# One VectorE operation in place of two ScalarE operations for each expert row of tokens 256 to 511

## The chip, the core and the metric

The kernel runs on one core of a Trainium2 chip. The metric is the time of one execution on the device in microseconds (us); lower is better. The engines are named as in the profile: PE is TensorE (PEld its weight loads), DVE is VectorE, ACT is ScalarE, POOL is GpSimd, SP is SyncE, which issues most of the weight transfers.

## What is computed

Two transformer blocks over 512 tokens of width 1024, in fp32. The first ends in a layer that looks up experts: each token chooses 128 of 16,384 experts (8 heads times 16), and takes from each one a row of `expert_u` and one of `expert_v`. The second block is a differential attention, an MLP, a latent attention (MLA), an MLP and a norm. The change lies in the expert layer:

```
ue = jnp.take(expert_u, expert, axis=0)
ve = jnp.take(expert_v, expert, axis=0)
h = jax.nn.gelu(jnp.einsum('thkd,td->thk', ue, xc).astype(F32), approximate=False)
return jnp.einsum('thk,thkd->td', (gate * h).astype(xc.dtype), ve)
```

`gate` is the softmax over the chosen experts' scores. For every token and expert one needs a dot product of 1024, a gelu, a product with the gate, and a row of 1024 added to the token's sum with that weight.

## The kernel before, in words

**Rows.** The expert layer is cut into 512 "rows". Row n gathers 128 experts at once, one for each of the 128 SBUF partitions: a 1 MB tile, 1024 numbers of u and 1024 of v in each partition. For rows 0 to 255 a row is one expert slot of 128 tokens. For rows 256 to 511 ("stacked") a row holds four expert slots of each of 32 tokens. A row goes through five steps, each on its own engine:

1. POOL issues the gather (`pool_rows`, L1754), once the buffer is free, which it is when PE has used the row seven before (row n-7) in it.
2. DVE makes the dot products (`dve_dot`, L1892), with a wait for the gather and for the dot of row n-1. One instruction gives 128 dot products, as a column of the tile `dots`.
3. ACT applies gelu (L1847), multiplies by the gate (L1849, "the weight"), and writes a diagonal matrix of the weights (L1856 for stacked rows: 128 x 32, four 32 x 32 diagonals one above the other; L1859 with 128 x 128 for the others). Each has a wait for the one before it. All three stand in `act_weight`.
4. PE multiplies the diagonal with the row's v part (`pe_rows`; L1778 for stacked rows, four matmuls of 128 x 32 by 128 x 256, which the trace shows as eight records). This adds the weighted v rows to the sums in PSUM. It is called acc(n) here, and the instruction of step 2 dot(n).
5. After 128 rows the sums are moved out and joined to the residual.

**What runs beside the rows.** Rows 0 to 255 run beside the choice of experts. Rows 256 to 511 run beside the whole second block for tokens 0 to 255 ("half 0"), which is the stage of the change. The second half of the tokens follows with no rows beside it. Each engine's program is written by generators: `beside(stage, rows, rate)` takes a piece of the second block's code, then as many steps of the row generator as are due (1.1 for each unit of weight), then the next piece. The same cut is made on every engine, so that each engine's stream is a fixed interleaving of row steps and pieces, and every engine works through its own in order. A place between two pieces at which row steps stand is called a gap here; a gap has one step, sometimes two, in the MLP one or none beside the half-weight pieces and now and then three.

**The row steps.** In step s DVE does dot(s+1), ACT does the three operations of row s+1, and PE does acc(s-1) for the stacked rows (`late`, with LAG = 1). So PE's part of a row stands two steps behind DVE's and ACT's part. Where the engines keep level, that is the slack that a row has between its diagonal and its use.

**The weights of the second block.** Matmuls of the second block run on weights that are split into two parts. SP loads 512 KB to a `raws` buffer, ACT writes the high part (`act_hi`, L297, 128 x 1024, to `whs` or `whw`), POOL subtracts it from the weight to get the low part (`pool_lo`, L303, to `wls` or `wlw`). POOL's stream has the low parts and the gathers in one fixed order, so that a gather waits behind the low parts that stand ahead of it, and these wait for ACT's high parts. PE's matmuls of the second block are at L1998 (projections), L2557 and L2576 (the two halves of the MLP), L2239 and others.

**The attentions.** In `attention` each of 16 blocks of queries goes round the engines: PE makes the scores, DVE the maximum (L2482, for MLA L2939), ACT the exponential (L2391, for MLA L2827), DVE the softmax's division (L2496, for MLA L2948), PE turns the block and multiplies with v, ACT and DVE put the result away. Between gelu and exponential ACT loads another table (ACT_TABLE_LOAD).

Two more DVE lines are spoken of: L2048 writes a diagonal (128 x 128, from `ident` in SBUF to SBUF, by TENSOR_SCALAR), and L2484 scales a single column.

## Time and profile before

| | |
|---|---|
| Time, median of 3 runs | 3049.65 us (3047.44 to 3058.9) |
| Time of the profiled execution | 3047.7 us, its span 3045.9 us |
| Busy over the span | PE 85%, PEld 64%, POOL 54%, DVE 58%, ACT 46% |
| Granted clock of PE over the span | 0.927 |
| HBM traffic | 787.84 MB read, 261 GB/s over the span |
| Stage of rows 0 to 255 | about 610 to 1283 us of the span |
| Stage of the change, rows 256 to 511 beside half 0 | 1283 to 2310 us |
| Half 1 alone | 2310 us to the end |

The span is the time from the profile's first instruction to its last; the 1.8 us between it and the execution's time lie around it. Busy shares are means over stages with different limits, so that the stage of the change has to be read by itself. The "chain of waits" is the profile's way back from the last instruction: at each step to what released it, or to the instruction ahead of it on its engine. In this profile it reaches back to 1557 us and no further.

### The profile page before, as it was taken

Reading aid. Unit: us, or ns where it says so; the run is one execution under the profiler, and the core shown is the slowest. Engines: PE = TensorE matmul, PEld = TensorE weight load, DVE = VectorE, ACT = ScalarE, POOL = GpSimd, SP = SyncE. Lnnn points to the kernel's source line nnn. Section 1 sums busy time; section 2 is a strip of 40 time slices with the busy share of each in tenths; the row PEclk is TensorE's granted clock in tenths of the full one; section 3 lists DMA queues with packets and bytes.
Section 4 is the critical chain, followed back from the end, with each engine's and each line's share of the span. In section 5 each row is a group of like instructions: output and inputs, shape, how many; then the busy total and the mean of one; then the engine's idle time right before and its main releaser. Section 6 shows DMA issues by size and latency. Waiting matters only on the chain. (4 is left out here: it accounts for less than half of the span.)

```text
span 3045.9 us, 49365 instructions
## 1 busy us (share of the span) xinstructions
PE 2585.2 (85%) x18974; PEld 1960.1 (64%) x18974; DVE 1763.8 (58%) x3863; ACT 1388.3 (46%) x3129; POOL 1648.2 (54%) x973
## 2 busy tenths in 40 slices
PE   6997977987877777687698997679997999999998
PEld 3865965743333232265477776458776979989998
DVE  5686433767777776765654457565446463256323
ACT  2231222243344343456865456765554454444543
POOL 3822113834444443466287776358883618852785
PEclk8988978999999999888799998889997999999999
DMA  7210013289999999779789997989995415542453
GB/s 293 101 59 26 4 57 152 93 331 421 421 421 421 421 421 415 316 300 401 284 325 401 377 389 296 376 314 393 402 409 218 152 34 175 187 134 74 157 186 115
DMA packets 140538, 797.61 MB, mean 262 GB/s; under 512 B 15504, under 2 KB 18704, under 8 KB 67600
## 3 DMA queue, kind: packets, MB, share of 16 engines
q0 software_dynamic: 73728, 536.90, 43.4%
q1 hardware_dynamic: 65856, 253.09, 23.3%
q10 hardware_dynamic: 720, 4.46, 0.3%
q8 instruction: 151, 2.47, 0.3%
q14 instruction: 83, 0.68, 0.1%
HBM read 787.84 MB, written 6.55 MB: 261 GB/s over the span
## 5 line engine op out<-in xcount | busy, mean ns | idle before, releaser
L303 POOL TENSOR_TENSOR wls<-raws,whs 128x1024 fp32r<-128x1024 f32 (+1 forms) x256 | 612.0, 2400 | 370.3 <-ACT whs L297 368.3
L1998 PE MATMUL ps<-ts,whs 128*128 128x256 f32 x1424 | 292.2, 306 | 27.5 <-DVE ts L2093 19.6
L1754 POOL DMA_INDIRECT raw<-in_peer_uv,un x205 | 209.3, 1021 | 191.7 <-PE ps L1778 87.6
L297 ACT CAST whs<-raws 128x1024 fp32r<-128x1024 f32 (+1 forms) x256 | 263.9, 1036 | 96.8 <-PE ps L2576 35.2
L303 POOL TENSOR_TENSOR wlw<-raws,whw 128x1024 fp32r<-128x1024 f32 x112 | 267.8, 2404 | 70.4 <-ACT whw L297 69.7
L1847 ACT ACTIVATE un<-un 128x1 f32<-128x1 f32 x384 | 77.6, 202 | 445.6 <-DVE scratch L1892 432.0
L1998 PEld LDWEIGHTS ps<-ts,whs 128*128 128x128 f32 x1424 | 239.6, 205 | 56.1 <-issue 26.8
L1892 DVE SCALAR_TENSOR_TENSOR scratch<-raw,ps 128x1024 f32<-128x1024 f32 x149 | 181.4, 1217 | 133.4 <-DMA raw<-in_peer_uv,un 120.2
L2576 PE MATMUL ps<-ts,whs 128*128 128x256 f32 x1216 | 228.7, 289 | 0.2 <-DVE ts L2629 0.2
L1998 PE MATMUL ps<-ts,wls 128*128 128x256 f32 x712 | 209.8, 295 | 0.0
L303 POOL TENSOR_TENSOR wl<-raw,wh 128x2048 fp32r<-128x2048 f32 x23 | 107.1, 4660 | 186.0 <-ACT wh L297 186.0
L2576 PEld LDWEIGHTS ps<-ts,whs 128*128 128x128 f32 x1216 | 190.6, 193 | 19.8 <-issue 16.8
L2557 PE MATMUL ps<-ts,whs 128*128 128x256 f32 x1088 | 202.3, 287 | 0.0
L2557 PE MATMUL ps<-ts,whw 128*128 128x256 f32 x960 | 182.6, 291 | 9.5 <-DVE ts L2093 9.5
L2658 DVE TENSOR_TENSOR kept<-kept,ps 128x256 f32<-128x256 f32 x256 | 103.8, 418 | 129.4 <-PE ps L2576 129.3
L2557 PEld LDWEIGHTS ps<-ts,whs 128*128 128x128 f32 x1088 | 170.3, 193 | 12.8 <-issue 11.9
L2576 PE MATMUL ps<-ts,wls 128*128 128x256 f32 x608 | 172.8, 284 | 0.0
L2557 PEld LDWEIGHTS ps<-ts,whw 128*128 128x128 f32 x960 | 152.5, 195 | 22.2 <-DVE ts L2093 10.7
L1892 DVE SCALAR_TENSOR_TENSOR scratch<-raw,scratch 128x1024 f32<-128x1024 f32 x108 | 135.6, 1260 | 50.4 <-DMA raw<-in_peer_uv,un 26.1
L1754 POOL DMA_INDIRECT un<-in_peer_uv,un x104 | 105.2, 1011 | 108.7 <-PE ps L1782 51.6
L333 PE MATMUL ps<-uh,wh 128*128 128x512 f32 x368 | 149.3, 406 | 15.3 <-DVE ul L1281 5.3
L2622 DVE SCALAR_TENSOR_TENSOR ps<-ps,rs 128x256 f32<-128x256 f32 x128 | 55.2, 431 | 179.2 <-PE ps L2557 178.9
(443 smaller groups left out, 6883.2 us busy)
## 6 DMA issues: line engine op xcount, KB each, us to landing
raws<-in_w_up SPq DMA_DIRECT2D x128, 512.0 KB, 4.2
raws<-in_w_down SPq DMA_DIRECT2D x128, 512.0 KB, 4.7
scratch<-in_ada_w SPq DMA_DIRECT2D x17, 1024.0 KB, 13.2
raws<-in_w_qk SPq DMA_DIRECT2D x32, 512.0 KB, 8.5
raw<-in_w_in SPq DMA_DIRECT2D x11, 1024.0 KB, 5.3
raw<-in_peer_w_q SPq DMA_DIRECT2D x8, 1024.0 KB, 8.0
raws<-in_w_v SPq DMA_DIRECT2D x16, 512.0 KB, 5.7
raws<-in_w_o_a SPq DMA_DIRECT2D x16, 512.0 KB, 4.0
```

The costliest lines, as they stand in the source:

```text
L297: e.copy(self.wh[h][:, 0:width], self.raw[slot][:, 0:width]).then_inc(*self.tick("hi", key))
L303: e.tensor_tensor(self.wl[h][:, 0:width], self.raw[slot][:, 0:width], self.wh[h][:, 0:width].bitcast(F32), ALU.subtract).then_inc(*self.ti ...
L333: ins = e.matmul(self.ps[:, b, :], l, r, start=k == 0 and i == 0, stop=k == nk - 1 and i == 2)
L1754: e.indirect_dma_start(self.rows[r], None, self.d["peer_uv"], index).then_inc(*self.tick(f"row{r}", n, 16))
L1847: e.activation(gelus[:, c], dots[:, c], ACT.Gelu, bias=0.0, scale=1.0).then_inc(*self.tick(S))
L1892: e.scalar_tensor_tensor(out=self.junk[0 if n < 128 else n % 2 if n < 256 else 1], in0=self.rows[r][:, 0:1024], scalar=1.0, in1=xn, op0=AL ...
L1998: ins = e.matmul(o[:, 0:256], l, r, start=k == 0 and i == 0, stop=k == nk - 1 and i == 2)
L2557: ins = e.matmul(o[:, 0:256], l, r, start=k == 0 and n == 0, stop=k == 7 and n == 2)
L2576: ins = e.matmul(o[:, 0:256], l, r, start=t == 0 and n == 0, stop=t == 3 and n == 2)
L2622: e.scalar_tensor_tensor(out=x, in0=x, scalar=0.0, in1=H.rs, op0=ALU.max, op1=ALU.mult).then_inc(*self.tick(S, ("ready", g, t)))
L2658: e.tensor_tensor(x, x, self.bh((P_, "v", g, j)), ALU.add).then_inc(*self.tick(S, ("x", g, j)))
```

## The change

For stacked rows ACT now does the gelu alone. A new function, `dve_diagonal`, lets DVE write the diagonals with one `tensor_scalar`: the stack of unit diagonals (`each32`) times the gelu's column times the gate's column. It is called in DVE's row step n, behind dot(n+1), and waits for the gelu of row n and for acc(n-4), whose diagonal lay in the same buffer. PE's acc(n) now waits for DVE's diagonal instead of ACT's. Rows 0 to 255 are as before.

```
--- before.py
+++ after.py
@@ -1770,7 +1770,7 @@
                 b = 4 if tt == 0 else 6
                 if k == 0 and tt >= 2:
                     e.wait_ge(*self.at(A_, ("sums", tt - 1)))
-                e.wait_ge(*self.at(A_, ("diag", n)))
+                e.wait_ge(*self.at(D_ if self.stacked(n) else A_, ("diag", n)))
                 if self.stacked(n):
                     g = k // 32
                     for c in range(4):
@@ -1844,6 +1844,9 @@
         S, c, k = "peer_act", slice(n % 128, n % 128 + 1), n % 128
         dots, gelus, weight = self.dots[n >= 128], self.gelus[n >= 128], self.weight[n >= 128]
         e.wait_ge(*self.at("peer_dve", ("dot", n)))
+        if self.stacked(n):
+            e.activation(gelus[:, c], dots[:, c], ACT.Gelu, bias=0.0, scale=1.0).then_inc(*self.tick(S, ("gelu", n)))
+            return
         e.activation(gelus[:, c], dots[:, c], ACT.Gelu, bias=0.0, scale=1.0).then_inc(*self.tick(S))
         e.wait_ge(*self.last(S))
         e.activation(weight[:, c], gelus[:, c], ACT.Identity, bias=0.0,
@@ -1851,13 +1854,8 @@
         if n >= 4:
             e.wait_ge(*self.at("peer_pe", ("acc", n - 4)))
         e.wait_ge(*self.at(S, ("weight", n)))
-        diag = self.diag[n >= 128][n % 4]
-        if self.stacked(n):
-            e.activation(diag[:, 0:32], self.each32, ACT.Identity, bias=0.0,
-                         scale=weight[:, c]).then_inc(*self.tick(S, ("diag", n)))
-        else:
-            e.activation(diag, self.C("ident"), ACT.Identity, bias=0.0,
-                         scale=weight[:, c]).then_inc(*self.tick(S, ("diag", n)))
+        e.activation(self.diag[n >= 128][n % 4], self.C("ident"), ACT.Identity, bias=0.0,
+                     scale=weight[:, c]).then_inc(*self.tick(S, ("diag", n)))
 
     def act_join(self, e, tt):
         b = 4 if tt == 0 else 6
@@ -1871,10 +1869,20 @@
         for n in range(-1, 512 + LAG):
             if n + 1 < 512:
                 self.dve_dot(e, n + 1)
+            if 0 <= n < 512 and self.stacked(n):
+                self.dve_diagonal(e, n)
             if n in (130, 386 + LAG):
                 for j in range(8):
                     self.dve_join(e, n // 128 - 1, j)
             yield
+
+    def dve_diagonal(self, e, n):
+
+        k = n % 128
+        e.wait_ge(*self.at("peer_act", ("gelu", n)))
+        e.wait_ge(*self.at("peer_pe", ("acc", n - 4)))
+        e.tensor_scalar(self.diag[1][n % 4][:, 0:32], self.each32, self.gelus[1][:, k:k + 1], self.gate[n // 128][:, k:k + 1],
+                        ALU.mult, ALU.mult).then_inc(*self.tick("peer_dve", ("diag", n)))
 
     def dve_dot(self, e, n):
         S, r = "peer_dve", self.row_of(n)
```

The lines behind the change move by up to 8: DVE's dot is L1900 in the changed kernel, the gelu of stacked rows L1848, the new operation L1884, MLA's lines 2939, 2941, 2946, 2948 and 2954 are L2947, L2949, L2954, L2956 and L2962.

ACT's stream in the first MLP, before (`un` holds dots, gelus, weights, gates and diagonals of these rows; `kept` the unit diagonals; `whs` and `whw` are high parts of weights):

```order
L1847 ACTIVATE un<-un 128x1 [waits s_peer_dve]
L1849 ACTIVATE un<-un 128x1 [waits s_peer_act]
L1856 ACTIVATE un<-kept,un 128x32 [waits s_peer_act,s_peer_pe]
L1847 ACTIVATE un<-un 128x1 [waits s_peer_dve]
L1849 ACTIVATE un<-un 128x1 [waits s_peer_act]
L1856 ACTIVATE un<-kept,un 128x32 [waits s_peer_act,s_peer_pe]
L297 CAST whs_81<-raws_72 128x1024 [waits s_mlp00_pe,s_raw5]
L1847 ACTIVATE un<-un 128x1 [waits s_peer_dve]
L1849 ACTIVATE un<-un 128x1 [waits s_peer_act]
L1856 ACTIVATE un<-kept,un 128x32 [waits s_peer_act,s_peer_pe]
L297 CAST whw_83<-raws_73 128x1024 [waits s_mlp00_pe,s_raw6]
```

The same place now (the x3 stands for the two gelus shown above ahead of `whs_81`, and one just before them):

```order
L297 CAST whs_79<-raws_71 128x1024 [waits s_mlp00_pe,s_raw4]
L1848 ACTIVATE un<-un 128x1 [waits s_peer_dve] x3
L297 CAST whs_81<-raws_72 128x1024 [waits s_mlp00_pe,s_raw5]
L1848 ACTIVATE un<-un 128x1 [waits s_peer_dve]
L297 CAST whw_83<-raws_73 128x1024 [waits s_mlp00_pe,s_raw6]
```

Two ACT instructions of every row are gone, and with them ACT's wait for PE in the rows; each high part still stands behind the gelu of the row ahead of it.

DVE's stream in MLA at a gap with two row steps, before (`me` is the exponential's result, `ts` the attention's result):

```order
L2948 TENSOR_SCALAR me_137<-me_137,kept 128x128 [waits s_mla0_dve]
L2954 TENSOR_TENSOR ts_90<-ps,ts_90 128x128 [waits s_mla0_act]
L1892 SCALAR_TENSOR_TENSOR scratch,un<-scratch,ps 128x1024 [waits s_row10,s_peer_pe,s_peer_dve]
L1892 SCALAR_TENSOR_TENSOR scratch,un<-un,ps 128x1024 [waits s_row4,s_peer_pe,s_peer_dve]
L2939 TENSOR_REDUCE kept<-ps 128x1 [waits s_mla0_pe]
L2941 TENSOR_SCALAR kept<-kept 128x1 [waits s_mla0_dve]
```

And the same gap now:

```order
L2956 TENSOR_SCALAR me_137<-me_137,kept 128x128 [waits s_mla0_dve]
L2962 TENSOR_TENSOR ts_90<-ps,ts_90 128x128 [waits s_mla0_act]
L1900 SCALAR_TENSOR_TENSOR scratch,un<-scratch,ps 128x1024 [waits s_row10,s_peer_pe,s_peer_dve]
L1884 TENSOR_SCALAR un<-kept,un 128x32 [waits s_peer_pe,s_peer_act]
L1900 SCALAR_TENSOR_TENSOR scratch,un<-un,ps 128x1024 [waits s_row4,s_peer_pe,s_peer_dve]
L1884 TENSOR_SCALAR un<-kept,un 128x32 [waits s_peer_pe,s_peer_act]
L2947 TENSOR_REDUCE kept<-ps 128x1 [waits s_mla0_pe]
L2949 TENSOR_SCALAR kept<-kept 128x1 [waits s_mla0_dve]
```

Each diagonal stands behind the dot of the next row, which waits for the next row's gather, and ahead of the next dot or of the maximum of the attention.

## Rows read from the trace of the kernel before

**Rows 1.** Waits, 1283 to 2310 us; columns: waiter, what ended it: us, times, longest.

```profile
ACT un L1847 <- DVE scratch L1892: 259.2, 164, 9.6
POOL wls L303 <- ACT whs L297: 129.9, 52, 14.9
PE ps L1778 <- ACT un L1856: 64.1, 43, 12.4
```

**Rows 2.** Windows; busy of PE, PEld, DVE, ACT, POOL, then clock, DMA share, GB/s.

```profile
1440.00:1500.00 60.00, 36.78 (x253) 23.14 (x249) 40.39 (x131) 57.29 (x140) 14.52 (x16) 0.80 0.77 285
1600.00:1800.00 200.00, 182.66 (x1556) 150.39 (x1555) 94.72 (x195) 102.73 (x249) 159.72 (x98) 0.97 0.99 393
1965.00:2010.00 45.00, 30.14 (x179) 18.30 (x180) 23.55 (x67) 38.82 (x90) 12.00 (x13) 0.73 0.76 275
600.00:1283.00 683.00, 533.20 (x1444) 228.32 (x1444) 507.37 (x1313) 269.06 (x819) 304.63 (x261) 0.96 0.97 399
```

**Rows 3.** Groups of instructions, 1283 to 2310 us: count | busy, mean ns | idle before.

```profile
L1856 ACT ACTIVATE un<-kept,un 128x32 f32<-128x32 f32 x256 | 82.3, 322 | 23.7
L1849 ACT ACTIVATE un<-un 128x1 f32<-128x1 f32 x256 | 75.5, 295 | 8.3
```

**Rows 4.** Chain of waits in the first MLP: start us, us, what.

```profile
1767.77 0.95 POOL un L1754
...
1771.31 9.40 DMA raw<-in_peer_uv,un
...
1782.10 0.21 ACT un L1847
...
1782.33 0.30 ACT un L1849
...
1782.72 0.04 ACT un L1856
...
1782.95 1.04 ACT whw L297
...
1784.06 2.39 POOL wlw L303
...
1786.59 0.95 POOL scratch L1754
```

**Rows 5.** Chain of waits in MLA.

```profile
1985.86 0.21 ACT un L1847
1986.09 0.30 ACT un L1849
...
1986.82 1.28 ACT L2827
```

**Rows 6.** Chain of waits, first and last pass over L1849; 28 in all.

```profile
1607.66 0.30 ACT un L1849
...
2290.52 0.30 ACT un L1849
```

**Rows 7.** ScalarE's gelu, 1440 to 1500 us: count: ns min/median/max.

```profile
L1847 ACT ACTIVATE un<-un x15: 186/202/203, 1443.7 to 1497.9; 128x1 f32<-128x1 f32 x15
```

**Rows 8.** Instructions in time, first MLP: acc(370) and dot(371).

```profile
1753.66 0.64 PE L1778 MATMUL ps<-un 128*32 128x256 f32 x8
1754.84 1.22 DVE L1892 SCALAR_TENSOR_TENSOR scratch<-raw,ps 128x1024 f32<-128x1024 f32 x1 [2.70 <-DMA raw<-in_peer_uv,un]
```

**Rows 9.** Instructions in time, MLA: acc(423), dot(424), dot(425).

```profile
1980.85 1.08 PE L1778 MATMUL ps<-raw,un 128*32 128x256 f32 x8 [1.35 <-ACT un L1856]
...
1983.34 1.21 DVE L1892 SCALAR_TENSOR_TENSOR scratch<-scratch,ps 128x1024 f32<-128x1024 f32 x1
...
1984.60 1.22 DVE L1892 SCALAR_TENSOR_TENSOR scratch<-un,ps 128x1024 f32<-128x1024 f32 x1
```

**Rows 10.** VectorE's TENSOR_SCALAR at two sizes: count: ns min/median/max.

```profile
L2484 DVE TENSOR_SCALAR kept<-kept x64: 153/154/155, 1414.3 to 2471.0; 128x1 f32<-128x1 f32 x64
L2048 DVE TENSOR_SCALAR diag<-kept x8: 273/674/2374, 1311.3 to 2346.8; 128x128 f32<-128x128 f32 x8
```

**Rows 11.** Instructions in time: two L2048 beside a low part of POOL.

```profile
1311.10 2.35 POOL L303 TENSOR_TENSOR wls<-raws,whs 128x1024 fp32r<-128x1024 f32 x1 [8.65 <-ACT whs L297]
...
1311.30 2.43 DVE L2048 TENSOR_SCALAR diag<-kept 128x128 f32<-128x128 f32 x2
```

More of the change, by code:

```diff
@@ L1772, in pe_rows @@
                     e.wait_ge(*self.at(A_, ("sums", tt - 1)))
-                e.wait_ge(*self.at(A_, ("diag", n)))
+                e.wait_ge(*self.at(D_ if self.stacked(n) else A_, ("diag", n)))
                 if self.stacked(n):
@@ L1846, in act_weight @@
         e.wait_ge(*self.at("peer_dve", ("dot", n)))
+        if self.stacked(n):
+            e.activation(gelus[:, c], dots[:, c], ACT.Gelu, bias=0.0, scale=1.0).then_inc(*self.tick(S, ("gelu", n)))
+            return
         e.activation(gelus[:, c], dots[:, c], ACT.Gelu, bias=0.0, scale=1.0).then_inc(*self.tick(S))
@@ L1853, in act_weight @@
         e.wait_ge(*self.at(S, ("weight", n)))
-        diag = self.diag[n >= 128][n % 4]
-        if self.stacked(n):
-            e.activation(diag[:, 0:32], self.each32, ACT.Identity, bias=0.0,
-                         scale=weight[:, c]).then_inc(*self.tick(S, ("diag", n)))
-        else:
-            e.activation(diag, self.C("ident"), ACT.Identity, bias=0.0,
-                         scale=weight[:, c]).then_inc(*self.tick(S, ("diag", n)))
+        e.activation(self.diag[n >= 128][n % 4], self.C("ident"), ACT.Identity, bias=0.0,
+                     scale=weight[:, c]).then_inc(*self.tick(S, ("diag", n)))
     def act_join(self, e, tt):
@@ L1873, in dve_rows @@
                 self.dve_dot(e, n + 1)
+            if 0 <= n < 512 and self.stacked(n):
+                self.dve_diagonal(e, n)
             if n in (130, 386 + LAG):
@@ L1877, in dve_rows, with dve_diagonal @@
             yield
+    def dve_diagonal(self, e, n):
+        k = n % 128
+        e.wait_ge(*self.at("peer_act", ("gelu", n)))
+        e.wait_ge(*self.at("peer_pe", ("acc", n - 4)))
+        e.tensor_scalar(self.diag[1][n % 4][:, 0:32], self.each32, self.gelus[1][:, k:k + 1], self.gate[n // 128][:, k:k + 1],
+                        ALU.mult, ALU.mult).then_inc(*self.tick("peer_dve", ("diag", n)))
     def dve_dot(self, e, n):
```

## The prediction

> **What bounds the kernel now.** I read the waits of the stage of the change first, then its windows, then the chain of waits, then single places in time. Outside 1283 to 2310 us nothing changes, so the argument is about these 1027 us.
>
> The waits show ACT standing 259.2 us at the gelu until DVE's dot is done, POOL 129.9 us at the low parts until ACT's high parts are done, and PE 64.1 us at acc until ACT's diagonal is there [rows 1]. The windows show that the stage has no single bound [rows 2]. In 1440 to 1500 us (differential attention) ACT is busy 57.29 of 60 us. In 1600 to 1800 us (first MLP) no engine is full: PE 182.66, POOL 159.72, ACT 102.73, DVE 94.72 of 200 us; but the DMA engines are busy 0.99 of the time at 393 GB/s. In 1965 to 2010 us (MLA) ACT has 38.82 of 45 us and DMA has room.
>
> The chain tells what ties the MLP together [rows 4]. A gather is issued at 1771.31 and takes 9.40 us; then come dot, gelu, weight and diagonal on ACT, the high part that stands behind them (1782.95), POOL's low part (1784.06), and the next gather, which stood behind it (1786.59). That is a ring through POOL, DMA, DVE, ACT and POOL, of 1786.59 - 1771.31 = 15.3 us for four rows, 3.8 us a row. The two operations that the change takes off ACT lie on it. In MLA the ring is shorter: dot on DVE, gelu, weight, diagonal on ACT, table load, exponential, and back [rows 5].
>
> **The change part by part.**
>
> *ScalarE loses the weight and the diagonal, 256 times.* Their busy time is 75.5 + 82.3 = 158 us [rows 3], but most of it lies beside other work. On the chain, what goes is the time from the weight's start to the start of what follows the diagonal: 1782.95 - 1782.33 = 0.62 us in the MLP [rows 4], 1986.82 - 1986.09 = 0.73 us in MLA [rows 5]. The chain passes over them 28 times between 1557 and 2310 us [rows 6]; ten of these lie in MLA. So 10 x 0.73 + 18 x 0.62 = **18.5 us** come off. Ahead of 1557 us the chain shows nothing. There I take the minute in which ACT is 95% busy [rows 2]: 15 rows [rows 7] x 0.67 us (the mean of the two) = **10 us**. Together 28.5 us, an upper bound as far as the chain goes.
>
> *VectorE gains one TENSOR_SCALAR of 128 x 32.* No such row exists. It lies between 0.153 us for one column and 0.273 us, the shortest for 128 columns [rows 10]; I take 0.2, nearer to the small one. 256 x 0.2 = 51 us of DVE work. In the MLP DVE idles 105 of 200 us [rows 2], so it is covered there; in MLA, at a gap with two rows, it lies between the two dots and so on the ring: ten passes x 0.2 = **2 us** lost. The whole 51 us would be the other end.
>
> *It can be blocked by POOL.* Two L2048 that start 0.2 us behind a low part's start take 2.43 us together, against 0.27 each when free: they end as the low part does (1313.45 and 1313.73) [rows 11]. So a diagonal that starts under a low part waits for its end, up to 2.4 us. With POOL's share of low parts a bit over half in the MLP (159.72 us less about fifty gathers of 0.95 is some 112 of 200 [rows 2, 4]), a start at random would wait 0.56 x 1.2 = 0.7 us, some 140 us over the 200 rows outside the attentions. I cost that at little, for two reasons: DVE's idle 105 us of 200 cover 37 us, and the start isn't random: the low part starts 2 us behind a dot's end (high part between), so it is over or nearly over when the next dot ends 3.8 us later. By the Trainium skill, page "SBUF — State Buffer", section "Who interferes with whom", a VectorE op of this kind and a GpSimd op exclude each other for a whole instruction, whichever came first. By that rule POOL would lose at most the diagonal's own 0.2 us whenever it comes second, 51 us of POOL's time if it always did, and the sum with all of that on the ring would be 28.5 - 51, a loss; no row of this trace shows POOL as the one that waits.
>
> *TensorE waits for something later.* acc(n) needed dot(n) and 1 us of ACT; now it needs dot(n+1), queued behind the gather of row n+1. In the MLP acc(370) started at 1753.66, dot(371) ended at 1756.06: 2.4 us too late [rows 8]. In MLA at the gap with two rows acc(423) started at 1980.85, and DVE was through with dot(424) at 1984.6 only [rows 9]: PE was a whole piece ahead and must now stay level. Does that cost? In the MLP PE has 17 us idle in 200, and its only customer, the gather seven rows on, is issued at 1767.77 [rows 4], 13.5 us after acc(370) ended at 1754.3. A shift of 3 us is paid once, not per row, as long as rows arrive no faster than PE takes them. I charge it each time a DMA-bound stretch gives way to a PE-bound one, half of about four times 2.7: **5 us**. In the attentions there are about twelve gaps with two rows, each with acc, scores, turn and product now behind the dot. ACT's table load, gelu and exponential run meanwhile, and I find some 0.5 us of PE's work left uncovered: **6 us**.
>
> *The memory system.* In the MLP DMA is full; 393 GB/s there against 399 over the long stretch of gathers alone [rows 2]. Of the passes there and in the stretches beside, about a dozen gain only what DMA gives, and the landing gets longer instead: half of 12 x 0.62 is **4 us** back.
>
> The sum: 28.5 - 2 - 5 - 6 - 4 = 11.5 us faster. Against the profiled execution's own 3047.7 us that is **3036 us**. That execution is 2 us below the median of 3049.65.
>
> A measurement of this kernel tells 0.5%, 15 us, from no change. Against the median that puts the bounds at 3034.4 and 3064.9.
>
> **The rivals.**
>
> *A. The forecast, 55%.* Gain on the rings, half of it given back. 3018 to 3048 us.
>
> *B. The full gain, 17%.* PE's waits stay hidden and the shorter ring makes the other idle places shrink as well: 3047.7 - 28.5 = 3019, down to 3010. For it: 64.1 us of PE's waits ended with ACT's diagonal, and ACT is the one engine at 95% in an attention. Against it: DMA at 0.99 in the MLP.
>
> *C. Nothing is left, 10%.* DMA sets the MLP's pace, and in the attentions the diagonal in DVE's stream costs what ACT saves: 3047 us.
>
> *D. Slower, 18%: PE loses its lead.* Where PE and the rows' arrival are level, every alternation costs. If the 2.4 us of the MLP [rows 8] are paid in one of ten of the 200 rows outside the attentions instead of four times, and a low part's blocking (1 us on the mean of those that meet it) comes on top, that is 20 x 3.4 = 68 us, less 28.5: 3047.7 + 39 = 3087. It decides from the point at which PE pays in more than 12 rows of the 256 (28.5 / 2.4). For it: PE is busy 91% in the MLP, so it catches up by only 0.3 us a row. Against it: the gather has 13.5 us of slack behind acc.
>
> **How the numbers follow.** The range holds A and B and the near part of D: 3010 to 3062. Faster by over 0.5%: B with its 17% and nearly half of A, 41%. Slower by over 0.5%: most of D, 14%. The rest, 45%, is within.
>
> **What would show it right or wrong.** In the profile after: gelu followed at once by the high part or the table load, with the chain no longer over any weight or diagonal of ACT; ACT under 90% in 1440 to 1500 us; the new L1884 at about 0.2 us with a tail to 2.4 under low parts; PE's waits at acc ended by DVE's diagonal and in sum not over 100 us; half 1 unchanged at about 736 us. Forecast A is wrong if the stage of rows 256 to 511 is longer than 1027 us, or shorter by more than 28 us. D is right if acc's waits pass 150 us, most of them in the MLPs; C if the stage is the same, and shorter attentions are lost again in the MLPs.

## The result, and the profile after

| | |
|---|---|
| Before, median of 7 runs | 3052.99 us (3044.93 to 3058.9) |
| Changed, median of 7 runs | 3081.79 us (3069.9 to 3092.49) |
| Ratio, 95% interval | 1.0098 (1.0075 to 1.0121) |
| Profiled execution, changed | 3069.9 us, span 3068.1 us, clock 0.927 |

The change makes the kernel slower by 1.0%, some 30 us. The profiled execution is the fastest of the seven and shows 22 us of them. Where a price is given below, it is the recorded ratio less 1, or the difference of two such ratios, times 3050 us. The ratio compares all runs of two kernels on the same chip and is not exactly the quotient of the medians that are shown; the expectations, written earlier, give prices as differences of medians, so that the kernel before with one wait more stands there with 14 us and here with 17.

The waits of the stage of the change, changed kernel (waiter, what ended the wait: us, times, longest):

```profile
ACT un L1848 <- DVE scratch L1900: 298.3, 152, 10.4
...
POOL wls L303 <- ACT whs L297: 148.2, 59, 14.4
PE ps L1778 <- DVE un L1884: 131.0, 72, 7.4
ACT ps L2614 <- DVE ps L2630: 127.4, 61, 4.9
...
DVE scratch L1900 <- DMA raw<-in_peer_uv,un: 46.5, 39, 4.9
```

Against [rows 1] ACT waits more for the dots (298.3 for 259.2) and POOL more for the high parts (148.2 for 129.9), though ACT has less to do. PE's wait at acc doubled, from 64.1 to 131.0 us. One row is new at this size: in the MLP, ACT's L2614, the step behind DVE's L2630 of the same tile, waits 127.4 us for it. In the kernel before the same two (there L2606 and L2622) stand in the grouped rows of the stage with 24.0 us of ACT's idle time:

```profile
L2606 ACT ACTIVATE ps<-ps 128x256 f32<-128x256 f32 x64 | 23.4, 366 | 24.0 <-DVE ps L2622 23.7
```

The windows of [rows 2] in the changed kernel, and the whole stage (busy of PE, PEld, DVE, ACT, POOL, then clock, DMA share, GB/s):

```profile
1440.00:1500.00 60.00, 42.12 (x286) 25.26 (x286) 48.38 (x166) 52.88 (x120) 15.62 (x17) 0.74 0.89 340
1600.00:1800.00 200.00, 181.53 (x1572) 150.15 (x1571) 137.80 (x251) 70.99 (x148) 161.72 (x100) 0.97 0.99 397
1965.00:2010.00 45.00, 27.60 (x187) 17.89 (x183) 24.08 (x77) 31.67 (x64) 11.25 (x12) 0.81 0.80 300
1283.00:2336.00 1053.00, 872.62 (x7008) 680.11 (x6998) 750.58 (x1506) 463.91 (x962) 671.74 (x434) 0.91 0.89 350
```

ACT fell to 52.88 of 60 us in the differential attention, as wanted. In the MLP, DVE went from 94.72 to 137.80 us of 200 for 56 instructions more (251 for 195): 0.8 us each. The new operation by itself:

```profile
L1884 DVE TENSOR_SCALAR un<-kept,un x256: 289/299/5168, 1300.4 to 2336.3; 128x32 f32<-128x32 f32 x128
its engine sat idle before it (us, times) until:
  ACT un L1848: 2.3, 4
who waited for it (us, times):
  PEld ps L1778: 160.0, 89
  PE ps L1778: 131.0, 72
```

The durations are minimum, median and maximum in ns. Half of them take 0.30 us and one takes 5.17; the sum is 204.0 us (page of the profile), so 204.0 - 256 x 0.299 = 127.5 us are something else than work. 109 of the 256 began while POOL was inside a low part; those took 1.25 us on the mean and hold 103 of the 127.5 us. The profile's chain of waits runs over L1884 for 53 us of the stage. The longest diagonal, in the MLP, as the timeline has it (start, duration, engine and line; most rows of PE left out):

```profile
1660.66 1.21 DVE L1900 SCALAR_TENSOR_TENSOR scratch<-raw,ps 128x1024 f32<-128x1024 f32 x1
...
1661.27 0.95 POOL L1754 DMA_INDIRECT un<-in_peer_uv,un  x1 [0.16 <-issue]
...
1661.80 5.17 DVE L1884 TENSOR_SCALAR un<-kept,un 128x32 f32<-128x32 f32 x1
...
1662.25 2.38 POOL L303 TENSOR_TENSOR wls<-raws,whs 128x1024 fp32r<-128x1024 f32 x1
...
1663.30 0.28 PE L2565 MATMUL ps<-ts,wlw 128*128 128x256 f32 x1
1664.58 2.34 POOL L303 TENSOR_TENSOR wlw<-raws,whw 128x1024 fp32r<-128x1024 f32 x1
1666.88 0.42 DVE L2630 SCALAR_TENSOR_TENSOR ps<-ps,rs 128x256 f32<-128x256 f32 x1
...
1667.02 1.08 PE L1778 MATMUL ps<-raw,un 128*32 128x256 f32 x8 [3.44 <-DVE un L1884]
...
1667.33 0.37 ACT L2614 ACTIVATE ps<-ps 128x256 f32<-128x256 f32 x1 [4.68 <-DVE ps L2630]
```

The diagonal comes 0.5 us into a gather's issue, and two low parts go by before it is done, at the moment the second one ends. PE stands idle 3.44 us for it. Behind it on DVE stands L2630 of half 0's own tile, whose matmuls (L2565) had ended at 1663.58, and ACT's L2614 behind that waits 4.68 us. This is one of the waits that the table above sums up to 127.4 us: half 0's work, which has nothing to do with rows or diagonals, held up in VectorE's queue. A run below shows how much of the 127.4 us is the holding.

The other thing to see is MLA, where GpSimd works 11.25 of 45 us (1965 to 2010 us), gathers' issues among it. The same view, at a gap with one row:

```profile
2001.74 1.21 DVE L1900 SCALAR_TENSOR_TENSOR scratch<-un,ps 128x1024 f32<-128x1024 f32 x1
2001.85 0.39 PE L2223 MATMUL ps<-mat,vm 128*128 128x128 f32 x2
2002.88 0.08 DVE L1900 DVE_READ_ACCUMULATOR scratch<-un,ps 128x1 f32 x1
2002.88 0.30 DVE L1884 TENSOR_SCALAR un<-kept,un 128x32 f32<-128x32 f32 x1
...
2003.22 0.64 PE L1778 MATMUL ps<-un 128*32 128x256 f32 x8 [0.99 <-DVE un L1884]
```

The diagonal takes its 0.30 us, and PE stands idle 0.99 us all the same, since the diagonal of row n lies behind the dot of row n+1. So the profile after offers two causes: VectorE's operation is **held** while GpSimd works (127.5 us, part of it on the path), and acc(n) is **tied** to dot(n+1). Beside them stands the operation's own 0.30 us, and the relief of ScalarE, which should have been a gain. The experiments price each.

### The profile page after: what moved, and what is told of

It reads as the page before. It is cut to its first block, busy times and chain, and to the rows that moved or that the text cites. A ratio compares the mean times of both kernels' runs of the same rounds, so it can differ in the third digit from the quotient of the medians.

```text
span 3068.1 us, 49109 instructions
## 1 busy us (share of the span) xinstructions
PE 2587.2 (84%) x18974; PEld 1960.4 (64%) x18974; DVE 1938.5 (63%) x4119; ACT 1234.3 (40%) x2617; POOL 1646.1 (54%) x973
## 4 chain that ended last, share of the span: by engine, by line
PE 46%; DVE 18%; DMA 17%; issue 5%; POOL 4%; ACT 4%; DVEq 0%; ACTq 0%; SPq 0%
PE ps L2584 9%; PE ps L2565 9%; PE ps L2006 7%; DMA raw<-in_peer_uv,un 6%; DVE scratch L1900 4%; PE ps L1782 4%; PE ps L872 4%; PE ps L333 3%; DMA raw<-in_peer_uv,scratch 3%; DMA un<-in_peer_uv,un 2%; DMA w<-in_peer_uv,scratch 2%; POOL wls L303 2%; PE ps L1778 2%; DVE un L1884 2%; POOL wlw L303 1%
## 5 line engine op out<-in xcount | busy, mean ns | idle before, releaser
L303 POOL TENSOR_TENSOR wls<-raws,whs 128x1024 fp32r<-128x1024 f32 (+1 forms) x256 | 612.3, 2401 | 388.1 <-ACT whs L297 385.5
L1900 DVE SCALAR_TENSOR_TENSOR scratch<-raw,ps 128x1024 f32<-128x1024 f32 x149 | 180.9, 1214 | 59.3 <-DMA raw<-in_peer_uv,un 46.5
L1884 DVE TENSOR_SCALAR un<-kept,un 128x32 f32<-128x32 f32 x256 | 204.0, 797 | 2.4 <-ACT un L1848 2.3
L2565 PE MATMUL ps<-ts,whs 128*128 128x256 f32 x1088 | 204.4, 289 | 0.0
L2565 PE MATMUL ps<-ts,whw 128*128 128x256 f32 x960 | 180.0, 288 | 8.0 <-DVE ts L2101 8.0
L2630 DVE SCALAR_TENSOR_TENSOR ps<-ps,rs 128x256 f32<-128x256 f32 x128 | 55.2, 431 | 205.0 <-PE ps L2565 204.6
L2565 PEld LDWEIGHTS ps<-ts,whs 128*128 128x128 f32 x1088 | 172.1, 195 | 13.5 <-issue 13.5
L1778 PE MATMUL ps<-raw,un 128*32 128x256 f32 x1192 | 104.8, 427 | 89.9 <-DVE un L1884 76.6
L1848 ACT ACTIVATE un<-un 128x1 f32<-128x1 f32 x256 | 51.4, 202 | 305.8 <-DVE scratch L1900 298.3
L1900 DVE SCALAR_TENSOR_TENSOR scratch<-raw,scratch 128x1024 f32<-128x1024 f32 x108 | 135.5, 1260 | 49.5 <-DMA raw<-in_peer_uv,un 24.7
L2565 PEld LDWEIGHTS ps<-ts,whw 128*128 128x128 f32 x960 | 150.2, 192 | 21.1 <-issue 10.3
```

The lines of the kernel that those rows point to most:

```text
L303: e.tensor_tensor(self.wl[h][:, 0:width], self.raw[slot][:, 0:width], self.wh[h][:, 0:width].bitcast(F32), ALU.subtract).then_inc(*self.ti ...
L1778: ins = e.matmul(o, self.diag[1][n % 4][:, 0:32], row[:, 1024 + 256 * c:1280 + 256 * c], start=k % 32 == 0, stop=k % 32 == 31)
L1884: e.tensor_scalar(self.diag[1][n % 4][:, 0:32], self.each32, self.gelus[1][:, k:k + 1], self.gate[n // 128][:, k:k + 1], ALU.mult, ALU.mul ...
L1900: e.scalar_tensor_tensor(out=self.junk[0 if n < 128 else n % 2 if n < 256 else 1], in0=self.rows[r][:, 0:1024], scalar=1.0, in1=xn, op0=AL ...
L2565: ins = e.matmul(o[:, 0:256], l, r, start=k == 0 and n == 0, stop=k == 7 and n == 2)
```

## Experiments: held or tied

```
         e.tensor_scalar(self.diag[1][n % 4][:, 0:32], self.each32, self.gelus[1][:, k:k + 1], self.gate[n // 128][:, k:k + 1],
-                        ALU.mult, ALU.mult)...
+                        ALU.mult, ALU.mult,
+                        accum_out=self.diag[1][n % 4][:, 64:65])...
```

> The changed kernel, in which VectorE's diagonal also writes out an accumulated value (one column that nobody reads); the order, the waits and what each engine does stay. Theory 'held': the loss comes from VectorE's diagonals being held while GpSimd is inside an instruction (109 of 256 began under a low part, 128 us over their free 0.30 us), and the Trainium skill (SBUF — State Buffer, Who interferes with whom) excepts this form from the shared ports. It expects the diagonals at 0.3 to 0.4 us wherever they start, no tail to 2 us, and 3040 to 3055 us, at least 25 us below the changed kernel. Theory 'tied': the loss comes from acc(n) having to come behind dot(n + 1), and so behind the gather of row n + 1. It expects 3070 us or more, the diagonals quick or not. If the form is held as well, the diagonals keep their mean of about 0.8 us and the run tells nothing of either.

Measured: 3050.26 us (median of 11), ratio 0.999 (0.9979 to 1.0002). The groups of the stage (busy, mean ns | idle before):

```profile
L1778 PE MATMUL ps<-raw,un 128*32 128x256 f32 x1192 | 103.5, 421 | 71.2 <-DVE un L1884 58.0 <-ACT un L1848 12.4
...
L1884 DVE TENSOR_SCALAR_CACHE_REDUCE un<-kept,un 128x32 f32<-128x32 f32 x256 | 77.5, 303 | 2.9 <-ACT un L1848 2.9
```

Not one of the 256 took over 0.32 us, though 117 began under a low part. With the holding gone, the whole loss is gone, as theory 'held' expected. PE's idle time ahead of acc, all its groups together, is still 116 us against 64 in the kernel before.

**The same with nothing left out.** VectorE reads the unit diagonals as 3 groups of 12 with a gap between, and writes 36 columns. `iota` gets the same diagonals a second time, with the gaps.

```
+        self.each36 = self.C("iota")[:, 64:103].rearrange("p (a b) -> p a b", b=13)[:, :, 0:12]
...
-        e.tensor_scalar(self.diag[1][n % 4][:, 0:32], self.each32, ...
+        e.tensor_scalar(self.diag[1][n % 4][:, 0:36], self.each36, ...
```

> The changed kernel with the same product and nothing left out, but VectorE's operation reads its diagonals as 3 groups of 12 columns out of 39 and writes 36 columns in one run. The Trainium skill (VectorE: DVE Perf Modes) gives the two-port mode only where the outermost counts of source and destination are both even or equal; 3 and 36 are neither. If that decides, the operation is not held, takes about 0.30 us as in the run with the accumulated value, and the time is that run's, 3045 to 3055 us. If it is held all the same (mean near 0.8 us), the time stays at 3075 to 3085 us.

Measured: 3049.12 us (median of 12), ratio 0.9998 (0.9985 to 1.0011).

```profile
L1885 DVE TENSOR_SCALAR un<-kept,un 128x36 f32<-128x36 f32 x256 | 78.3, 306 | 2.9 <-ACT un L1849 2.9
```

Four columns more, the same engine, order and waits: the mean is 306 ns and the longest 0.31 us. What the changed kernel has beyond this one is that its operation is held: 1.0098 - 0.9998, some 30 us. The rule of the Trainium skill that the expectation draws on ("VectorE: DVE Perf Modes", "What auto-detection actually checks") agrees with the changed kernel and this one: with 3 and 36 as outermost counts nothing is held, with 32 and 32 it is. Other counts were not run. The waits of its stage tell which of the signs above belong to the holding:

```profile
ACT un L1849 <- DVE scratch L1901: 319.9, 168, 10.4
...
PE ps L1779 <- DVE un L1885: 105.4, 65, 7.4
...
ACT ps L2615 <- DVE ps L2631: 84.8, 59, 4.5
```

This kernel takes the time of the kernel before, and yet ACT waits even longer for the dots, and most of the new wait for L2630 (L2631 here) and of PE's wait at acc is still there. So about 43 of the 127.4 us and 26 of the 131.0 us came with the holding. The rest is an engine with less to do that waits more, or the tie. The chain of waits runs over the operation for 11 us here, against 53.

**The tie alone.** The kernel before, with one wait more:

```
                 e.wait_ge(*self.at(A_, ("diag", n)))
+                if self.stacked(n) and n < 511:
+                    e.wait_ge(*self.at(D_, ("dot", n + 1)))
```

> The kernel before with one wait more: TensorE's acc(n) of a stacked row also waits for dot(n + 1), as it has to in the changed kernel, while ScalarE makes the diagonal as ever and VectorE has no further work. Theory 'tied': 3070 us or more (18 us or more above the kernel before: what the change lost, 29 us, and part of what it should have gained), and the sum of TensorE's idle time ahead of the acc's at 120 us or more against 64. Theory 'held': at most 8 us above the kernel before.

Measured: 3065.15 us (median of 6), ratio 1.0056 (1.0038 to 1.0073): 17 us. Both expectations were missed, "tied" by a little and "held" by more. PE's idle time ahead of acc is 121 us in all, as "tied" had it. The waits of its stage:

```profile
PE ps L1780 <- DVE scratch L1894: 117.5, 76, 12.1
```

The tie is real and costs 17 us by itself. What it cannot do alone is explain the changed kernel's loss, since that kernel has the tie, has ScalarE's relief against it, and comes out even when nothing is held.

**The operation alone, held and not held.** The kernel before, with VectorE's operation added behind dot(n+1) into columns that nobody reads; then the same in the form with the accumulated value.

```
             if n + 1 < 512:
                 self.dve_dot(e, n + 1)
+            if 256 < n < 512:
+                self.dve_spare(e, n)
...
+    def dve_spare(self, e, n):
+        k = n % 128
+        e.wait_ge(*self.at("peer_act", ("weight", n)))
+        e.tensor_scalar(self.diag[1][n % 4][:, 64:96], self.each32, self.gelus[1][:, k:k + 1], self.gate[n // 128][:, k:k + 1],
+                        ALU.mult, ALU.mult).then_inc(*self.tick("peer_dve", ("spare", n)))
```

> The kernel before with the changed kernel's operation of VectorE added behind dot(n + 1), into columns that nobody reads, for rows 257 to 511; ScalarE still makes the diagonals that TensorE uses. Its cost can only go through VectorE: the dot of row n + 2 stands behind an operation that is held. Theory 'held': the operation means 0.7 to 0.9 us with a tail to 5 us, and the time is 5 to 20 us above the kernel before. Theory 'tied': within 5 us of the kernel before, since VectorE sat idle for a third of the stretch and no acc waits for the operation.

Measured: 3075.1 us (median of 5), ratio 1.0075 (1.006 to 1.009), 23 us, a little above the range of 'held' and far from that of 'tied'.

> The kernel before with VectorE's added operation (into columns that nobody reads) in the form with an accumulated value, which was never held. With the held form this cost 24 us. Theory 'held': the operation means 0.30 us and costs little, 0 to 8 us above the kernel before, so that 16 us or more of the 24 are the holding. If an operation more on VectorE costs in any form: 15 us or more above the kernel before, and the holding is the smaller part.

Measured: 3049.91 us (median of 11), ratio 1.0006 (0.9995 to 1.0017), 2 us. The two operations in the groups of their stage, the held form first:

```profile
L1885 DVE TENSOR_SCALAR un<-kept,un 128x32 f32<-128x32 f32 x255 | 236.7, 928 | 4.6 <-ACT un L1849 4.6
```

```profile
L1885 DVE TENSOR_SCALAR_CACHE_REDUCE un<-kept,un 128x32 f32<-128x32 f32 x255 | 77.0, 302 | 7.2 <-ACT un L1849 7.2
...
L1885 DVE DVE_READ_ACCUMULATOR un<-kept,un 128x1 f32 x255 | 21.0, 82 | 0.0
```

Nobody waits for this operation, and its work is covered: 77.0 + 21.0 us of VectorE cost nothing that can be measured. Held, it costs 21 us more, all of it through what stands behind it in VectorE's queue. In the changed kernel PE waits for it as well, and there the holding costs 30 us.

**Another order.** The changed kernel with the diagonal of row n ahead of dot(n+1), held and not held (the second again without the gate):

```
-            if n + 1 < 512:
-                self.dve_dot(e, n + 1)
             if 0 <= n < 512 and self.stacked(n):
                 self.dve_diagonal(e, n)
+            if n + 1 < 512:
+                self.dve_dot(e, n + 1)
```

> The changed kernel (held form) with VectorE's diagonal of row n ahead of dot(n + 1) in place of behind it. The tie is gone, the holding stays. Theory 'held': 3070 us or more, the diagonals' mean still 0.7 us or more. Theory 'tied': 3055 us or less.

> The run with the accumulated value (3050 us, the diagonals never held), with one move: VectorE makes the diagonal of row n ahead of dot(n + 1), not behind it. acc(n) is then free of the gather of row n + 1, and dot(n + 1) has to wait for ScalarE's gelu(n). By the price of the tie from the run with the wait (+14 us), 'tied is what is left': 3030 to 3040 us. If instead VectorE's wait for the gelu (some 0.5 us for each row whose gather is there) comes to cost as much as the tie: 3045 to 3060 us.

Measured: 3062.79 us (median of 6), ratio 1.0052 (1.0033 to 1.0071), held; 3046.32 us (median of 12), ratio 0.9992 (0.9979 to 1.0006), not held. The holding costs 18 us in this order too:

```profile
L1884 DVE TENSOR_SCALAR un<-kept,un 128x32 f32<-128x32 f32 x256 | 232.4, 908 | 22.9 <-ACT un L1848 21.2 <-issue 1.4
```

The first landed between its two expectations. Its diagonals are held for even longer than the changed kernel's (908 ns for 797), yet it is 14 us faster. That fits a price of holding that depends on who waits for the operation and not on its length alone; 18 us against 30 is hardly beyond what the intervals allow, so it is not shown. The second came out as its rival expectation had it: it was to gain what the tie cost and gained nothing to speak of (0.9992 against 0.999). Without the tie, VectorE waits 28.0 us for the gelus with the dots behind it, where it waited 2.9 in the changed kernel's order: one wait seems to have taken the place of the other.

```profile
L1884 DVE TENSOR_SCALAR_CACHE_REDUCE un<-kept,un 128x32 f32<-128x32 f32 x256 | 76.8, 300 | 29.6 <-ACT un L1848 28.0 <-issue 1.3
```

**More distance.** LAG 2 in place of 1 should leave the tie a step of slack. It was run on the form that is not held (without the gate), and on the kernel before as a control.

> The run with the accumulated value (3050 us), with TensorE's acc one step later (LAG 2 in place of 1). The tie to dot(n + 1) then has a step of slack: 3035 to 3045 us if the tie costs 14 us here too. Against it: the buffers of rows come free a step later, and the gathers, which wait for acc's in many steps, with them; if those decide, it is 3050 to 3070 us, with more idle time ahead of the dots.

> The kernel before with the acc's one step later (LAG 2), a control for the run that combined LAG 2 with the accumulated form and came out 58 us slower than with LAG 1. If it is the buffers of rows, which come free a step later, this run is 40 to 70 us above the kernel before as well; if it was the tie or VectorE's operation that went badly with the lag, it is within 15 us of the kernel before.

Measured: 3108.97 us, ratio 1.0206 (1.0181 to 1.0232), and 3138.59 us, ratio 1.0296 (1.0279 to 1.0313). Both are slower than any expectation had it. A step more costs the kernel before 90 us. The dots of the `raw` buffers stand idle longer for their gathers. First the kernel before, then the control, whose view ends at 2336 us with 140 of its 149 dots (up to its last row at 2405 us the wait for these gathers is 186 us, against 120):

```profile
L1892 DVE SCALAR_TENSOR_TENSOR scratch<-raw,ps 128x1024 f32<-128x1024 f32 x149 | 181.4, 1217 | 133.4 <-DMA raw<-in_peer_uv,un 120.2 <-PE ps L1800 6.1 <-PE ps L1778 5.2
```

```profile
L1892 DVE SCALAR_TENSOR_TENSOR scratch<-raw,ps 128x1024 f32<-128x1024 f32 x140 | 170.5, 1218 | 181.6 <-DMA raw<-in_peer_uv,un 166.8 <-PE ps L1778 8.2 <-PE ps L1800 5.9
```

More distance costs far more than the tie. That it does so through buffers that come free a step later is argued and not shown: the dots wait longer for their gathers, but the gathers' own wait for an acc did not grow (136 us against 150), and the granted clock of the stage fell from 0.91 to 0.87, which may be a cause or a consequence. The tied kernel loses less by the lag (1.0206 against 0.999, 66 us) than the kernel before, so some of the tie may find its slack, but it is no way out.

## Experiments: the relief, and a version that gains

**ScalarE relieved of the gate, nothing else.** The kernel before, in which the diagonal is scaled by the gelu itself (the gate is left out for rows 256 to 511).

```
-        e.activation(weight[:, c], gelus[:, c], ACT.Identity, bias=0.0,
-                     scale=self.gate[n // 128][:, k:k + 1]).then_inc(*self.tick(S, ("weight", n)))
+        if self.stacked(n):
+            weight = gelus
+        else:
+            e.activation(weight[:, c], ...
```

> The kernel before in which ScalarE leaves out the multiplication by the gate for rows 256 to 511 and scales the diagonal by the gelu itself; the result lacks the gate for those rows. It gives about half of the relief of ScalarE (82 us of its 158 us) with no new work or wait anywhere. If the chain's passes over ScalarE's weight were time, as the prediction's 28.5 us had it, the weights' part of it (0.32 us and the turn-round, some 0.4 us of each 0.67) is 15 to 20 us: 3033 to 3038 us. If the time in those passes was covered by other work, or the gathers decide: within 5 us of the kernel before.

Measured: 3031.42 us (median of 5), ratio 0.9933 (0.9919 to 0.9947): 20 us gained by one of the two operations, where 15 to 20 were expected and the other account allowed 5. This bears out the forecast's reading of the chain.

**With the tie, and with the unheld operation, on top of the relief.** Both still without the gate:

```
 (relief, and)
+                if self.stacked(n) and n < 511:
+                    e.wait_ge(*self.at(D_, ("dot", n + 1)))
```

> The run without ScalarE's gate (3031 us, the gate left out for rows 256 to 511) with the wait of acc(n) for dot(n + 1), which alone cost 14 us. 'Additive': 3045 us. If the tie costs more once ScalarE is quicker, because the wait for the dot is then the last one in more rows: 3050 us or more. If less: 3040 or less.

Measured: 3051.37 us (median of 12), ratio 1.0008 (0.9993 to 1.0023), just inside '3050 us or more'.

```
 (relief, and)
+            if 256 < n < 512:
+                self.dve_spare(e, n)
...
+        e.tensor_scalar(self.diag[1][n % 4][:, 64:100], self.each36, self.gelus[1][:, k:k + 1], self.gate[n // 128][:, k:k + 1],
+                        ALU.mult, ALU.mult).then_inc(*self.tick("peer_dve", ("spare", n)))
```

> The run without ScalarE's gate (3031 us, the gate is left out for rows 256 to 511 here too) with VectorE's added operation in the uneven form, which is not held, into columns that nobody reads. On the kernel before the added operation cost nothing when it was not held. 'Additive': 3031 us again, up to 3035. 'The operation takes the cover of the relief': 3038 to 3048 us, which would also say why VectorE's multiplication two rows ahead gave 3042 and not 3031.

Measured: 3036.23 us (median of 8), ratio 0.9969 (0.9956 to 0.9983), between the two expectations. Once ScalarE is relieved, the tie costs 1.0008 - 0.9933, 23 us (17 alone), and the operation 0.9969 - 0.9933, 11 us (2 alone). By the intervals the operation's rise (11 us, uncertain by 6, against 2, uncertain by 3) stands, while the tie's may be none. I read the first as cover that is gone: as long as ScalarE is late, 0.31 us of VectorE's beside it cost nothing.

**VectorE's product made early.** The gate doesn't depend on the dot. VectorE multiplies the unit diagonals by it two rows ahead, ScalarE scales that by the gelu; nothing is left out, and no acc is tied to a dot.

```
+            if self.stacked(n + 2) and n + 2 < 512:
+                self.dve_gated(e, n + 2)
...
+    def dve_gated(self, e, n):
+        k, tile = n % 128, self.diag[1][n % 4]
+        (waits for ScalarE's diagonal n - 4, at the start for acc(n - 4))
+        e.tensor_scalar(tile[:, 64:96], self.each32, self.gate[n // 128][:, k:k + 1], None,
+                        ALU.mult, ALU.add, accum_out=tile[:, 96:97]).then_inc(*self.tick("peer_dve", ("gated", n)))
...
+            e.activation(tile[:, 0:32], tile[:, 64:96], ACT.Identity, bias=0.0,
+                         scale=gelus[:, c]).then_inc(*self.tick(S, ("diag", n)))
```

> The kernel before, nothing left out, with ScalarE's multiplication by the gate replaced: VectorE multiplies the stack of diagonals by the gate two rows ahead (the form with an accumulated value, so that it is not held), and ScalarE scales that by the gelu. ScalarE is relieved of 0.32 us a row as in the run without the gate (3031 us), no acc is tied to a dot, and VectorE has 0.3 us a row more to do. Expected: 3030 to 3040 us, faster than both kernels. If VectorE's added work costs through the dots, 3045 us or more.

Measured: 3042.43 us (median of 12), ratio 0.9974 (0.9955 to 0.9992), a gain, but short of the 3030 to 3040 us expected. Then four rows in one operation of two operands:

```
-            if self.stacked(n + 2) and n + 2 < 512:
+            if self.stacked(n + 2) and n + 2 < 512 and n % 4 == 2:
                 self.dve_gated(e, n + 2)
...
+        e.tensor_tensor(tiles, self.each32.unsqueeze(1).to_broadcast([128, 4, 32]),
+                        self.gate[n // 128][:, k:k + 4].unsqueeze(2).to_broadcast([128, 4, 32]),
+                        ALU.mult).then_inc(*self.tick("peer_dve", ("gated", n)))
```

> The kernel before with ScalarE's multiplication by the gate replaced as in the run that has VectorE do it two rows ahead, but for four rows in one operation (two operands in SBUF, 128 columns), 64 operations in place of 256. The operation costs VectorE perhaps 0.3 us, and as it reads two operands from SBUF it may be held by a low part: at 0.8 us each that is 51 us on VectorE, at 0.3 us 19 us, against 77 us. Expected 3030 to 3043 us, the run without the gate (3031 us) being the floor. If single long waits on VectorE cost as much as many short ones: 3045 us or more.

Measured: 3043.18 us (median of 12), ratio 0.9982 (0.9969 to 0.9995), at the upper end of its range and no better. And the first again, with the 3 groups of 12 columns in place of the accumulated value:

```
-        e.tensor_scalar(tile[:, 64:96], self.each32, self.gate[n // 128][:, k:k + 1], None,
-                        ALU.mult, ALU.add, accum_out=tile[:, 96:97])...
+        e.tensor_scalar(tile[:, 64:100], self.each36, self.gate[n // 128][:, k:k + 1], None, ALU.mult)...
```

> VectorE multiplies the diagonals by the gate two rows ahead, as in the run that gave 3042 us, nothing left out, but in the uneven form and so without the read of the accumulator (0.08 us) behind each of the 256. If VectorE's time is what kept that run from 3031 us, it gains in proportion, some 3 of its 11 us: 3036 to 3041 us. If the place of the operation is what costs, 3042 us as before.

Measured: 3034.58 us (median of 5), ratio 0.9958 (0.9944 to 0.9971): 13 us faster than the kernel before and 43 us faster than the changed one, a little under the 3036 to 3041 us expected. The new operation in the three:

```profile
L1891 DVE TENSOR_SCALAR_CACHE_REDUCE un<-kept,un 128x32 f32<-128x32 f32 x256 | 61.9, 242 | 0.0
...
L1891 DVE DVE_READ_ACCUMULATOR un<-kept,un 128x1 f32 x256 | 21.0, 82 | 0.0
```

```profile
L1893 DVE TENSOR_TENSOR un<-kept,un 128x128 f32<-128x128 f32 x64 | 58.3, 912 | 4.4 <-PE ps L1782 4.4
```

```profile
L1892 DVE TENSOR_SCALAR un<-kept,un 128x36 f32<-128x36 f32 x256 | 62.8, 245 | 0.0
```

The one without the accumulator's read spends 62.8 us on VectorE against 82.9. That the 20 us of difference are worth 5 us of time fits with what the added operation cost under the relief, but the intervals of the two ratios overlap, so that it is VectorE's time is likely and not shown.

## Why the prediction was wrong

The forecast was 3036 us; it is 3082, outside the range and on the other side. The changed kernel's 30 us, put together from the runs:

| term | forecast | measured | from |
|---|---|---|---|
| ScalarE's relief, gate | | -20 | relief run |
| ScalarE's relief, diagonal | | -15 | not measured: what is left of the sum |
| both, with what the memory system takes | -28.5 + 4 | -35 | not measured: the 3 x 12 form's 0 less the two rows below |
| VectorE's operation, not held | +2 | +11 | on top of the relief |
| acc tied to dot(n+1) | +5 +6 | +23 | on top of the relief |
| VectorE's operation held | little | +30 | changed kernel against the 3 x 12 form |
| sum | -11.5 | +30 | |

Each measured difference carries some 4 to 8 us of uncertainty. The diagonal's share closes the sum, is uncertain by some 10 us, and rests on it that the prices of the tie and of the operation, each taken on top of half of the relief, add up. It was not run by itself; a kernel in which nobody writes these diagonals, as nobody applies the gate in the relief, would have shown it.

*"I cost that at little": the step that failed.* The forecast had the mechanism, the row that shows it [rows 11], and even the size: "some 140 us" if starts fell at random, against 127.5 measured. Charged at little, it cost 30 us of time. The forecast argued the cost away twice. First, the starts weren't random, since the low part would be over when the next dot ends. They came out as random starts would: in the stage POOL is busy 671.74 us, of which 252 gathers' issues of 0.95 leave 432 for low parts, 41% of 1053 us, and 109 of 256 diagonals, 43%, began under one. One ring read from four rows [rows 4] was taken for the phase of all rows. Second, "DVE's idle 105 us of 200" would cover it. Idle time covers an operation's time only if nothing is due behind it while it runs. The timeline above shows L2630 due at 1663.58 and begun at 1666.88. The spare operation shows it cleanly: 98 us of VectorE's work cost 2 us, some 160 us of holding cost 21 more.

*The bound of one low part.* The forecast gave "up to 2.4 us" for a held diagonal. Eight took over 2.5 us, the longest 5.17: before seven of them a second low part went ahead, and the eighth waited for the end of a gather's issue and a low part behind it.

*The operation's own time.* 0.2 us was taken, between 0.153 and 0.273 [rows 10]; it is 0.299 with 32 columns and two factors. With 36 columns it is 0.306 with two factors and 0.245 with one, so the second factor costs, and the bounds had only rows with one. The place where it was charged, ten gaps of MLA, was too few: on top of the relief it costs 11 us.

*The tie.* 11 us were charged, 23 measured (17 without the relief). "A shift of 3 us is paid once" holds only within one stretch. The start of dot(n), against the kernel before, counted in each trace from dot(0), in us (single executions: their last row has 10.0 for the tie's 17 and 23.5 for the changed kernel's 30):

| row n | place | tie alone | relief alone | changed, 3 x 12 form | changed |
|---|---|---|---|---|---|
| 311 | end of the differential attention | +3.3 | -8.4 | -2.9 | 0.0 |
| 330 | | +7.3 | -7.1 | +4.3 | +11.2 |
| 412 | start of MLA | +2.5 | -11.0 | -2.5 | +12.9 |
| 434 | end of MLA | +7.5 | -19.0 | -2.5 | +12.2 |
| 446 | | +11.6 | -19.2 | +2.6 | +19.3 |
| 511 | | +10.0 | -21.3 | +0.2 | +23.5 |

The relief gains 6 us in the differential attention (rows 286 to 311) and 8 us in MLA: the places that the forecast named. The tie takes 5 us in MLA and 4 more just behind each attention; behind the first attention it is given back in the MLP, in MLA and behind it it stays. So it was paid more than once, and the four alternations at half of 2.7 us were too little. The holding is the difference of the last two columns: 2.9 us up to row 311, 12.5 more up to row 412, nothing in MLA (-0.7) and 8.6 behind it. It is paid outside the attentions, most of it in the MLPs, where the low parts are.

*The signs the forecast had named.* ACT under 90% in 1440 to 1500 us: 88%. The chain no longer over ACT's weight or diagonal: so it is. L1884 at 0.2 us with a tail to 2.4: 0.30 and 5.17. PE's waits at acc not over 100 us: 131.0. Half 1 unchanged: dot(511) is 23.5 us later than before and the last instruction 21.7. *Rival D*, slower, gave 3087 us, close to the 3082, but by another mix: it put 2.4 us of PE's lead and 1 us of holding into each of twenty rows, and asked for acc waits past 150 us. Of the two it was the holding that decided, and without it the change would have been no change at all, which is the size that rival C gave, though by DMA's pace and not by the tie.

*The Trainium skill's rule* on the shared ports ("SBUF — State Buffer", "Who interferes with whom") was used in the forecast for POOL's side only. On that side nothing shows: the mean of the low parts to `wls` over the whole span is 2401 ns in the changed kernel and 2400 before. It was VectorE that came second. That the first to issue keeps the ports fits the low parts, but not three diagonals that began just before one and were held (last section); the profile's start of an instruction may lie ahead of its claim on the ports.

## What to carry to other kernels

When an operation moves to VectorE beside a GpSimd that works in SBUF, find out whether its form can be held, and if so count a random start and ask what is queued behind it. Here VectorE's idle time covered 98 us of added work (2 us of time), but not 160 us of holding (21 us more). A form that is not held (here an uneven grouping of the source, four columns wider) took the whole 30 us away, though it made no gain by itself. And move the part that is known early: the factor that didn't depend on the dot could be made two rows ahead, where hardly anything waits for it (2.1 us in all), and that half of the change was worth 13 us where the whole of it cost 30.

## What was unexpected of the hardware

- A `tensor_scalar` that waits for GpSimd is not next in line: in the timeline above two low parts of 2.38 and 2.34 us followed each other directly, both began after the diagonal (1661.80), and it ended with the second. Nor is it enough to start first: three diagonals that began 0.06 to 0.07 us before a low part ended with it, after 2.5 us.
- The end of a gather's issue on GpSimd (0.95 us) holds a diagonal too, the rest of it does not. In the changed kernel's trace 53 began inside an issue that no low part followed at once. The seven with 0.33 to 0.49 us of the issue left took 0.33 to 0.50 us and ended within 0.02 us of its end; the twenty with 0.57 us or more left took 0.30 us. It adds up to under 1 us here.
- The `tensor_tensor` of two SBUF operands, 128 x 128, took 279 ns at least and 4780 at most, 912 on the mean: reading two operands from SBUF it is held as the `tensor_scalar` is (32 of the 64 took over 0.35 us), and one held operation in place of four unheld ones gained nothing.
- A product by two column factors takes 0.306 us for 36 columns where one factor takes 0.245.
